# Streaming both halves of the activations as one operand in the q, k and u projections of a fused two-layer decoder trunk

## The reference

```python
h = rmsnorm(x, norm_pre_mix[layer])
# layer 0: one projection into u, va, q, k, vb (1024 columns each)
z = h @ w_in
a_out = gelu(u) * (tril(w_s) @ layernorm(gelu(va)) + b_s)
b_out = dilated_mixture(q * HEAD_DIM ** -0.5, k, vb)      # 8 heads of 128
y = concatenate([a_out, b_out]) @ w_out
# layer 1: q, k, v = split(h @ w_in, 3), 16 heads, stick-breaking attention
x = x + rmsnorm(y, norm_post_mix[layer])
h = rmsnorm(x, norm_pre_ffn[layer])
x = x + rmsnorm(square(relu(h @ w1)) @ w2, norm_post_ffn[layer])
```

## Time and profile before

| | |
|---|---|
| median of three runs | 2182.2 us |
| the profiled execution | 2182.25 us |
| its span, first to last instruction | 2180.4 us |
| TensorE busy | 2163.5 us (99%) |
| VectorE, ScalarE busy | 57%, 47% |
| mean granted clock of TensorE | 0.999 |

### The profile page before, as it was taken

One profiled execution on the slowest core, in us unless ns is written; L12 is line 12 of the kernel. 1 busy time (PEld: TensorE's weight loads), 2 busy tenths in 40 slices (PEclk: granted clock), 3 DMA queues, 4 the chain that ended last, 5 costly groups with the idle time before them and its releaser, 6 DMA issues.

```text
span 2180.4 us, 30479 instructions
## 1 busy us (share of the span) xinstructions
PE 2163.5 (99%) x12017; PEld 1891.5 (87%) x12017; DVE 1236.5 (57%) x1187; ACT 1016.1 (47%) x1097; POOL 18.7 (1%) x22
## 2 busy tenths in 40 slices
PE   9999999999999999999999999999999999999998
PEld 7999888888888888888899999888888888888886
DVE  5556567555554555555655555566545645554555
ACT  5444345543443443454535545564434534443543
POOL 0000000000000000000000000000000000000000
PEclk9999999999999999999999999999999999999999
DMA  9555555566556556655454555555566565656553
GB/s 310 188 174 174 194 174 156 182 203 193 189 187 191 183 193 212 192 192 193 155 194 155 173 173 188 170 156 184 191 194 192 175 211 174 199 192 210 187 193 116
DMA packets 202768, 406.73 MB, mean 187 GB/s; under 512 B 6400, under 2 KB 7744, under 8 KB 202176
## 3 DMA queue, kind: packets, MB, share of 16 engines
q1 hardware_dynamic: 202272, 405.37, 57.3%
q10 hardware_dynamic: 416, 0.23, 0.0%
HBM read 403.47 MB, written 2.10 MB: 186 GB/s over the span
## 4 chain that ended last, share of the span: by engine, by line
PE 96%; DVE 2%; issue 0%; ACT 0%; DMA 0%; POOL 0%; POOLq 0%; DVEq 0%; SPq 0%; ACTq 0%
PE ps L1061 96%; DVE w_lo L652 1%; DVE act_pair L700 0%; PE ps L1145 0%; DVE tmp L730 0%; DVE x_sb L692 0%; DMA w_raw<-in_ab_w_in_dram 0%; POOL rst L327 0%; ACT act_pair L389 0%; PE ps L1217 0%; ACT tmp L428 0%; ACT w_hi L357 0%; DVE tmp L954 0%; PE ps L1196 0%; DVE bn L995 0%
## 5 line engine op out<-in xcount | busy, mean ns | idle before, releaser
L652 DVE TENSOR_TENSOR w_lo<-w_raw,w_hi 128x1024 fp32r<-128x1024 f32 x752 | 914.2, 1225 | 832.9 <-ACT w_hi L357 822.5
L357 ACT ACTIVATE w_hi<-w_raw 128x1024 fp32r<-128x1024 f32 x752 | 789.6, 1059 | 997.4 <-PE ps L1061 992.0
L1061 PE MATMUL ps<-act_pair,w_hi 128*128 128x256 f32 (+1 forms) x3968 | 854.4, 337 | 0.5 <-issue 0.4
L1061 PEld LDWEIGHTS ps<-act_pair,w_hi 128*128 128x128 f32 x3968 | 664.6, 190 | 64.4 <-issue 1.7
L1061 PE MATMUL ps<-act_pair,w_lo 128*128 128x256 f32 x2944 | 557.4, 283 | 0.0
L1061 PE MATMUL ps<-w_hi,hid_hi 128*128 128x512 f32 x1280 | 499.9, 391 | 0.0
L1061 PE MATMUL ps<-w_hi,hid_lo 128*128 128x512 f32 x1280 | 498.1, 389 | 0.0
L1061 PE MATMUL ps<-w_lo,hid_hi 128*128 128x512 f32 x1280 | 498.0, 389 | 0.0
L1061 PEld LDWEIGHTS ps<-act_pair,w_lo 128*128 128x128 f32 x2944 | 457.6, 191 | 18.7
L1061 PEld LDWEIGHTS ps<-w_hi,hid_lo 128*128 128x128 f32 x1280 | 240.2, 188 | 50.3
L1061 PEld LDWEIGHTS ps<-w_hi,hid_hi 128*128 128x128 f32 x1280 | 240.3, 188 | 49.3
(11 more groups left out here) (108 smaller groups left out, 573.7 us busy)
## 6 DMA issues: line engine op xcount, KB each, us to landing
w_raw<-in_ffn_w_dram SPq DMA_DIRECT2D x256, 1024.0 KB, 5.3
w_raw<-in_sb_w_in_dram SPq DMA_DIRECT2D x48, 1024.0 KB, 5.1
w_raw<-in_ab_w_in_dram SPq DMA_DIRECT2D x39, 1024.0 KB, 5.1
w_raw<-in_ab_w_out_dram SPq DMA_DIRECT2D x16, 1024.0 KB, 5.1
w_raw<-in_sb_w_out_dram SPq DMA_DIRECT2D x16, 1024.0 KB, 5.1
gpost<-in_norm_post_mix_dram SPq DMA_DIRECT2D x2, 1024.0 KB, 7.3
gpost<-in_norm_post_ffn_dram SPq DMA_DIRECT2D x2, 1024.0 KB, 6.8
out_dram<-x_sb SPq DMA_DIRECT2D x3, 512.0 KB, 2.7
```

What stands on the lines that cost most here:

```text
L357: nc.scalar.activation(w_hi[:, t % RING, :, :], w_raw[:, t // 2, h:h + 2, :], ACT.Copy).then_inc(hi_ready, 1)
L652: nc.vector.tensor_tensor(w_lo[:, t % RING, :, :], w_raw[:, t // 2, h:h + 2, :], w_hi[:, t % RING, :, :].bitcast(F32), ALU.subtract).then_ ...
L1061: return nc.tensor.matmul(dst, lhsT, rhs, start=start, stop=stop, skip_group_check=True)
```

## The change

The units of u, of q and k of layer 0, and of q and k of layer 1 except the first q become pair units: tick_pairs now takes its first bank. Their posts get the two steps more: ScalarE's `rest` (semaphore a_rest) and VectorE's `add_rest` (semaphore a_sum), then the scaling. Since a set now has four banks and only 0 to 5 are free, sets overlap: units 2 and 3 have 4 to 7 and 0 to 3; q and k have 2 to 5 and 0 to 3 in the first group of layer 0, 0 to 3 and 2 to 5 in all others. Where the set overlaps that of the unit before, the unit is a `pair_unit`: its first two ticks are computed for one pair of banks, then for the other; ahead of the second pair it waits for the earlier sum (or, for q in layer 1, for v's post). Both ticks are signalled in the second half. v moves to banks 4 and 5 in the first group and 0 and 1 after; OUT_BUF turns by one, and the last `take` and the sums of squares read its banks. TensorE transposes the scales ahead of tick 5 in place of 4, and VectorE copies them at tick 6 of the first unit in place of before its tick 1. keep_busy uses bank 0 throughout.

Left out below: the renamings from `par` to `4 * par` in the MLP and tick_pairs, the `extras` argument of the MLP's `up`, and the new bank index in the two `transition` calls.

```diff
...
-OUT_BUF = [0, 1, 2, 0]
+OUT_BUF = [1, 2, 0, 1]
...
+        a_rest, a_sum = sem("a_rest"), sem("a_sum")
...
-            def qkv_group(u, extras):
-                for i in range(3):
-                    unit(u + i, nothing, {t - 8 * i: f for t, f in extras.items() if 8 * i < t < 8 * i + 8})
+            def rest(u, dst, first):
+                unit_finished(u)
+                nc.scalar.activation(dst[:, :, :], bank4_halves(first)[1], ACT.Copy).then_inc(a_rest, 1)
+            def qkv_group(u, extras, q_bank, k_bank):
+                posts = (lambda: rest(u, qT, q_bank), lambda: rest(u + 1, kT, k_bank), nothing)
+                for i, post in enumerate(posts):
+                    unit(u + i, post, {t - 8 * i: f for t, f in extras.items() if 8 * i < t < 8 * i + 8})
...
+            def post_u(j):
+                rest(2 + j, (qT, kT)[j], 4 - 4 * j)
+                gelu_u(j)
...
-                unit(2 + j, lambda j=j: gelu_u(j))
-            qkv_group(4, {m + 2: [lambda m=m: gate_hi(m)] for m in range(4)})
-            qkv_group(7, l0_extras(0))
+                unit(2 + j, lambda j=j: post_u(j))
+            qkv_group(4, {m + 2: [lambda m=m: gate_hi(m)] for m in range(4)}, 2, 0)
+            qkv_group(7, l0_extras(0), 0, 2)
...
-            qkv_group(U_IN1, {9: [suffix_matrices]})
+            unit(U_IN1, nothing)
+            unit(U_IN1 + 1, lambda: rest(U_IN1 + 1, kT, 2), {1: [suffix_matrices]})
+            unit(U_IN1 + 2, nothing)
...
-                qkv_group(U_IN1 + 3 * g, l1_extras(g - 1))
+                qkv_group(U_IN1 + 3 * g, l1_extras(g - 1), 0, 2)
...
-                if k:
-                    scale_tiles(k)
...
-            def qkv_group(u, extras):
+            def add_rest(dst, first, n):
+                dve.wait_ge(a_rest, n)
+                nc.vector.tensor_tensor(dst[:, :, :], bank4_halves(first)[0], dst[:, :, :], ALU.add).then_inc(a_sum, 1)
+                dve.wait_ge(a_sum, n)
+            def scaled_q(src):
+                nc.vector.scalar_tensor_tensor(qT[:, :, :], src, SCALE, rs_tiles, ALU.mult, ALU.mult
+                                               ).then_inc(post_done, 1)
+            def post_k(first, n):
+                add_rest(kT, first, n)
+                nc.vector.tensor_tensor(kT[:, :, :], kT[:, :, :], rs_tiles, ALU.mult).then_inc(post_done, 1)
+            def post_v(u, buf):
+                unit_finished(u)
+                for b in range(TB):
+                    last = nc.vector.tensor_scalar(v_sb[:, b, :], ps[:, 2 * buf + b, :], rst[:, 6 + b:7 + b], None,
+                                                   ALU.mult)
+                last.then_inc(post_done, 1)
+            def qkv_group(u, extras, q_bank, k_bank, v_buf, n):
                 def post_q():
-                    unit_finished(u)
-                    nc.vector.scalar_tensor_tensor(qT[:, :, :], bank2_tiles(0), SCALE, rs_tiles, ALU.mult, ALU.mult
-                                                   ).then_inc(post_done, 1)
-                def post_k():
-                    unit_finished(u + 1)
-                    nc.vector.tensor_tensor(kT[:, :, :], bank2_tiles(1), rs_tiles, ALU.mult).then_inc(post_done, 1)
-                def post_v():
-                    unit_finished(u + 2)
-                    for b in range(TB):
-                        last = nc.vector.tensor_scalar(v_sb[:, b, :], ps[:, 4 + b, :], rst[:, 6 + b:7 + b], None, ALU.mult)
-                    last.then_inc(post_done, 1)
-                for i, post in enumerate((post_q, post_k, post_v)):
+                    add_rest(qT, q_bank, n)
+                    scaled_q(qT[:, :, :])
+                for i, post in enumerate((post_q, lambda: post_k(k_bank, n + 1), lambda: post_v(u + 2, v_buf))):
...
-                for j in range(4):
-                    up(0, j // 2, j % 2, fresh=j == 0)
+                up(0, 0, 0, fresh=True, extras={6: [lambda: scale_tiles(2 * layer + 1)]})
+                for j in range(1, 4):
+                    up(0, j // 2, j % 2)
...
-                unit_finished(2 + j)
-                nc.vector.tensor_tensor((qT, kT)[j][:, :, :], bank2_tiles(j), rs_tiles, ALU.mult).then_inc(post_done, 1)
+                dst = (qT, kT)[j]
+                add_rest(dst, 4 - 4 * j, j + 1)
+                nc.vector.tensor_tensor(dst[:, :, :], dst[:, :, :], rs_tiles, ALU.mult).then_inc(post_done, 1)
...
-            qkv_group(4, gates)
-            qkv_group(7, l0_extras(0))
+            qkv_group(4, gates, 2, 0, 2, 3)
+            qkv_group(7, l0_extras(0), 0, 2, 0, 5)
...
-            qkv_group(U_IN1, {})
+            def first_q():
+                unit_finished(U_IN1)
+                scaled_q(bank2_tiles(0))
+            unit(U_IN1, first_q, {6: [lambda: scale_tiles(2)]})
+            unit(U_IN1 + 1, lambda: post_k(2, 7))
+            unit(U_IN1 + 2, lambda: post_v(U_IN1 + 2, 0))
...
-                qkv_group(U_IN1 + 3 * g, l1_extras(g - 1))
+                qkv_group(U_IN1 + 3 * g, l1_extras(g - 1), 0, 2, 0, 2 * g + 6)
...
-                keep_busy(0 if k == 2 else 2, 6)
+                keep_busy(0, 6)
...
-                if k and s == 4:
+                if k and s == 5:
...
-            def qkv_group(u, extras, fresh=None):
-                for i, tick in enumerate((tick_features, tick_features, tick_tokens)):
-                    unit(u + i, tick, i, fresh=fresh if i == 0 else None,
-                         extras={t - 8 * i: f for t, f in extras.items() if 8 * i <= t < 8 * i + 8})
+            def pair_unit(u, first, halves, extras, second_free):
+                pe.wait_ge(post_done, u - 1)
+                for n, half in enumerate(halves):
+                    for f in extras.get(n, []):
+                        f()
+                    if n:
+                        second_free()
+                    pe.wait_ge(hi_ready, 8 * u + 2)
+                    for kt in range(4):
+                        for f in half:
+                            mm(ps[:, first + f, :], w_hi[:, kt // 2, kt % 2, f * P:(f + 1) * P], act_pair[:, kt, :, :],
+                               kt == 0, False)
+                    pe.wait_ge(lo_ready, 8 * u + 2)
+                    for kt in range(4):
+                        for f in half:
+                            last = mm(ps[:, first + f, 0:T], w_lo[:, kt // 2, kt % 2, f * P:(f + 1) * P],
+                                      act_hi[:, kt, :], False, False)
+                        if n and kt % 2:
+                            last.then_inc(pe_ticks, 1)
+                for s in range(2, TICKS):
+                    for f in extras.get(s, []):
+                        f()
+                    tick_pairs(first, s, s % RING, act_hi, act_lo, 8 * u + s + 1)
+            def part_extras(extras, i):
+                return {t - 8 * i: f for t, f in extras.items() if 8 * i <= t < 8 * i + 8}
+            low, high = (0, 1), (2, 3)
+            def summed(n):
+                pe.wait_ge(a_sum, n)
...
-            unit(2, tick_features, 0)
-            unit(3, tick_features, 1)
-            qkv_group(4, {1 + m: [lambda m=m: mix(m)] for m in range(4)})
-            qkv_group(7, l0_extras(0))
+            pe.wait_ge(s_scales, 1)
+            pe.wait_ge(s_prep, 3)
+            unit(2, tick_pairs, 4)
+            unit(3, tick_pairs, 0)
+            pair_unit(4, 2, (high, low), {1 + m: [lambda m=m: mix(m)] for m in range(4)}, lambda: summed(2))
+            pair_unit(5, 0, (low, high), {}, lambda: summed(3))
+            unit(6, tick_tokens, 2)
+            extras = l0_extras(0)
+            unit(7, tick_pairs, 0, extras=part_extras(extras, 0))
+            pair_unit(8, 2, (high, low), part_extras(extras, 1), lambda: summed(5))
+            unit(9, tick_tokens, 0, extras=part_extras(extras, 2))
...
-            qkv_group(U_IN1, {}, fresh=2)
+            unit(U_IN1, tick_features, 0, fresh=2)
+            pe.wait_ge(s_scales, 3)
+            unit(U_IN1 + 1, tick_pairs, 2)
+            unit(U_IN1 + 2, tick_tokens, 0)
             with pe.Fori(1, L1_GROUPS) as g:
-                qkv_group(U_IN1 + 3 * g, l1_extras(g - 1))
+                u, extras = U_IN1 + 3 * g, l1_extras(g - 1)
+                pair_unit(u, 0, (high, low), part_extras(extras, 0), lambda: pe.wait_ge(post_done, u))
+                pair_unit(u + 1, 2, (high, low), part_extras(extras, 1), lambda: summed(2 * g + 6))
+                unit(u + 2, tick_tokens, 0, extras=part_extras(extras, 2))
...
```

More of the change, by code:

```diff
@@ L150, in bank2, with bank4_halves @@
             return ps[:, 2 * b:2 * b + 2, :]
-        def bank4_halves(par):
-            set4 = ps[:, 4 * par:4 * par + 4, :]
+        def bank4_halves(first):
+            set4 = ps[:, first:first + 4, :]
             return set4[:, :, 0:T], set4[:, :, T:2 * T]
@@ L519, in ready @@
                         act.wait_ge(pe_ticks, 8 * u0 + 32)
-                transition(k, u0 + 4, [ps[:, b, :] for b in range(TB)], ready)
```

(21 more changed lines are left out.)

## The result

The changed kernel takes 2192.88 us (median of five runs, 2191.45 to 2195.82) against 2182.2: a ratio of 1.0047, 95% interval 1.0035 to 1.006. A second set of five gave 2191.53 (2189.74 to 2194.58), ratio 1.0046 (1.0032 to 1.006). Each ratio compares all runs of a kernel with all runs of the kernel before beside it, so it is not the quotient of the medians to the last digit. It is slower, as forecast, and by about twice the forecast amount; 2192.88 lies just outside the range.

What follows compares the result with a forecast made beforehand. TensorE, busy 2163.5 of 2180.4 us at full clock, was taken as the bound. 11.8 us off (matmuls, scales) against 17.1 on (waits, restarts) gave net +5.3 on 2182.25: forecast 2187.5 us, range 2178 to 2192.

Steps and rivals of the forecast that it cites:

- The matmuls: 13 feature units become pair units with fewer instructions, 0.72 us off each, 9.4 us off in all.
- The scales: Scale transposes moved to tick 5 lose their wait at k = 1 and 3; w_lo is late next; 2.4 us off.
- The new post chain: Cut q and k units wait for the previous unit's post: 0.1, 1.0, 1.1, 3.4 and 8.5 us on.
- rival 2: Only plain waits come, ScalarE's late conversion not reaching the sum and the transposes keeping their slack: 2176.3 us; 11%.
- rival 1: The halves of the cut units hide the post, no wait of consequence: 2170.5 us; 6%.
- A second wait in unit 8: Tick 0's late signal delays ScalarE's conversion and the chain to the normalising; TensorE waits 2.3 us at the transposes.
- Restarts: First matmuls behind each of some nine TensorE waits run slower, 0.08 us a wait, 0.7 us on.
- Rival 3: TensorE's clock falls to half rate behind idle stops, priced at 8 to 10 us; 8%.
- The sign for it: A dip of the profile's clock line in the changed trace was to show that the prediction is wrong.

Runs made afterwards that it cites:

- run with the short logs: Changed kernel with zeros written in place of absolute value, exponent and logarithm for layer 1's second pair of heads: 2180.29 us, ratio 0.9993.
- kernel with 6 and 5 zero products: Changed kernel with 6 zero matmuls ahead of the sum's wait in layer 1's three k units, 5 ahead of unit 8's transposes: 2188.46 us, ratio 1.0028.

## Why the prediction was wrong in size

- **The matmuls**: right. 0.69 us a unit measured for 0.72; 13 units give 9.0 us for 9.4. A pair tick of the changed kernel takes 1253.70 - 1250.90 = 2.80 us, for 2.79.
- **The scales**: right, 2.2 us for 2.4, and the new wait for w_lo was where it was placed.
- **The new post chain**: right. 0.97, 1.11, 3 x 1.18 and 3 x 2.77 us for 1.0, 1.1, 3 x 1.14 and 3 x 2.8. The run with the short logs showed that k's wait is ScalarE's queue; rival 2 needed q's sum in time and is out, as is rival 1.
- **A second wait in unit 8**: right, 2.32 us for 2.3. That its cause is the order behind the late signal of tick 0 is shown by moving the exponent.
- **Restarts**: 0.7 put in, somewhat too little. The wide block behind a wait takes 1.94 to 1.98 us at full clock, against 1.84 in the earlier trace rows: 0.1 a wait, some 1.0 for nine. That closes the sum: 2182.2 - 11.2 + 16.3 + 1.0 = 2188.3, the level without falls, 0.8 above the forecast.
- **Rival 3, the clock falls**: this is the step that failed. It was held apart from the sum at 8%, so that the sum had the clock at nothing, and priced at 8 to 10 us with a return of some 5 us that no row shows. It happens in at least nine of the ten runs of the changed kernel, behind some of the long waits, not behind all: ten runs lie 1.4 to 7.5 us above 2188.3 (the lowest, 2189.74, may be the start's stretch alone). A fall cost 1.4 to 1.5 us in the profiles, for the 2.6 guessed. The kernel with 6 and 5 zero products, equal in its waits' ends, shows none of it. So 2187.5 as the sum of work and waits was off by 0.8; the rest, 3.2 and 4.6 us in the two medians, is two to three falls, the start's own among them. A fair forecast would have put about one or two falls into the sum, since the only stops that rows showed as harmless were half as long.
- **The sign for it was blind.** The prediction read the full clock off and named a dip of that line as the sign. A character of it stands for 55 us, and a stretch of 3.4 us at half clock doesn't change a 9. The line of the changed kernel's page, with both stretches in it:

```profile
PEclk9999999999999999999999999999999999999999
```

That the clock stayed full across the wait of 1.5 us at k = 1 is true, but it takes a short stretch of the kernel before to show it:

```profile
362.00:370.00 8.00, 6.66 (x56) 6.46 (x55) 7.93 (x9) 2.60 (x3) 3.48 (x2) 1.00 0.16 33
```

The Trainium skill (TensorE: Matmul & The Clock Gate, Part 1) says that an idle array is put to half rate and that activity lifts it; these runs agree, with 0.50 granted behind 2.62 us of idle. They add that it doesn't happen every time: behind four of nine stops of 2.8 us in the profiles, by the times behind some of 2.3 us, and, outside the start phase, behind none of 1.0 to 1.2 us.

## What to carry to other kernels

When a bound engine is to gain waits, price each wait twice: its length, and the slower matmuls that may follow it; here a stop of 2.8 us cost 4.3 where the clock fell behind it (2.77, the restart's 0.1 and the fall's 1.4). Before cutting a unit to fit the banks, look for the assignment of banks that needs no cut, even if fewer units take the better form: eight whole units gave 5.5 us, thirteen with nine cut cost 8.3 (2188.3 - 2180.0), the falls not counted. And look for falls in stretches of a few us about each wait, not in a line of 40 slices. Last, a cut that delays a buffer's release is felt not at the buffer but at whatever is queued behind the refill on the other engine: here the exponent behind the conversion of tick 4, and through it the transposes.

## What the hardware showed unexpectedly

- Filling a wait with matmuls of a zero operand kept the granted clock at full behind all six filled waits of 2.8 us that profiles show (1.00 for 0.50 at the last k) and took 3.1 to 4.4 us off the median, without any work done sooner.
- A product of two plain float32 operands of 256 columns showed as two matmuls, 24 for 12, and took 0.42 us.
- The runs of one kernel lie on steps of some 1.4 to 1.7 us. The kernel before has two such levels, which go with a stretch of half clock near 11 us, so a single run of it can mislead by 1.4 us, beside the 2.2 that the scales' edit is worth; a single run of the changed kernel can by 6.
